# One 512-column up product per tile in an expert loop, with the transposes of the next token rows ahead of those of the hidden rows

## The reference, cut to what matters

```
def expert_block(args):
    xb, e = args
    hb = jax.nn.silu(xb @ w_gate[e]) * (xb @ w_up[e])
    return hb @ w_down[e]
```

## Time and profile before

| | |
|---|---|
| three executions | 2432.01, 2435.06, 2433.85 us |
| median | 2433.85 us |
| profiled execution, first to last instruction | 2431.3 us |
| TensorE busy | 2224.0 us, 91% of the span |
| weight loads of TensorE | 1827.0 us, 75% |
| VectorE, ScalarE, GpSimd busy | 1337.8, 909.3, 606.1 us |
| mean granted TensorE clock | 0.959 of full |
| expert loop | about 847 to 2296 us of the span |

### The profile page before, as it was taken

The page is one execution under the profiler, slowest core; times in us unless marked ns, Lnnn a source line. Parts: engine busy times, 40 slices in busy tenths (PEclk is TensorE's granted clock), DMA queues, the critical chain, the costliest instruction groups (busy, mean ns, idle before and its releaser), DMA issues.

```text
span 2431.3 us, 36221 instructions
## 1 busy us (share of the span) xinstructions
PE 2224.0 (91%) x12032; PEld 1827.0 (75%) x12033; DVE 1337.8 (55%) x2246; ACT 909.3 (37%) x1335; POOL 606.1 (25%) x672
## 2 busy tenths in 40 slices
PE   8999899999998299999999999999999999999700
PEld 3443778878886288888898898888888988988600
DVE  3221348888878555444544544554445455444298
ACT  2221123223333245434534534534345345443143
POOL 1000035454444412111211111111212111111166
PEclk9999999999999599999999999999999999999955
DMA  5980233333433377665765765865667678656386
GB/s 217 289 281 0 80 143 128 126 127 119 142 123 122 124 232 235 182 183 172 241 184 170 245 180 169 241 198 164 178 177 236 189 223 245 181 173 174 78 297 239
DMA packets 128121, 438.13 MB, mean 180 GB/s; under 512 B 24624, under 2 KB 26672, under 8 KB 123952
## 3 DMA queue, kind: packets, MB, share of 16 engines
q1 hardware_dynamic: 88736, 301.72, 35.5%
q0 software_dynamic: 39344, 135.88, 22.5%
HBM read 326.33 MB, written 112.26 MB: 180 GB/s over the span
## 4 chain that ended last, share of the span: by engine, by line
PE 91%; POOL 3%; issue 3%; DVE 2%; DMA 1%; ACT 0%; SPq 0%; POOLq 0%; DVEq 0%
PE ps L859 37%; PE ps L889 18%; PE ps L746 15%; PE ps L683 5%; PE ps L845 3%; POOL fin_r L1489 3%; PE ps L728 2%; PE ps L702 2%; PE ps L780 2%; PE ps L852 2%; PE ps L637 1%; PE ps L767 1%; PE ps L687 1%; PE ps L646 1%; PE ps L742 0%
## 5 line engine op out<-in xcount | busy, mean ns | idle before, releaser
L1246 DVE TENSOR_TENSOR wgu_lo<-wraw,wgu_hi 128x1024 fp32r<-128x1024 f32 x256 | 299.6, 1221 | 176.0 <-ACT wgu_hi L981 156.5
L859 PE MATMUL ps<-wgu_hi,mxT_hi 128*128 128x256 f32 (+1 forms) x1920 | 338.9, 319 | 1.6 <-DVE mxT_lo L1276 1.6
L859 PE MATMUL ps<-wgu_lo,mxT_hi 128*128 128x256 f32 (+1 forms) x1920 | 337.8, 318 | 0.0
L859 PE MATMUL ps<-wgu_hi,mxT_lo 128*128 128x256 f32 (+1 forms) x1920 | 337.8, 318 | 0.0
L859 PEld LDWEIGHTS ps<-wgu_hi,mxT_hi 128*128 128x128 f32 x1920 | 290.9, 191 | 33.7 <-issue 2.4
L859 PEld LDWEIGHTS ps<-wgu_lo,mxT_hi 128*128 128x128 f32 x1920 | 285.3, 191 | 25.0
L859 PEld LDWEIGHTS ps<-wgu_hi,mxT_lo 128*128 128x128 f32 x1920 | 285.3, 191 | 24.9
L981 ACT CAST wgu_hi<-wraw 128x1024 fp32r<-128x1024 f32 x256 | 253.6, 1062 | 20.3 <-DMA wraw<-expert_w_up 20.3
L1289 DVE TENSOR_TENSOR hid<-sgate,ps 128x256 f32<-128x256 f32 x160 | 67.2, 420 | 337.0 <-PE ps L859 337.0
L1456 POOL DMA_INDIRECT sums<-yrow,sx x81 | 131.4, 1622 | 296.4 <-DVE yrow L1303 270.9
L1004 ACT CAST hidT_hi<-ps 128x256 fp32r<-128x256 f32 x160 | 59.6, 372 | 381.7 <-PE ps L852 381.7
(11 more groups left out here) (175 smaller groups left out, 3373.3 us busy)
## 6 DMA issues: line engine op xcount, KB each, us to landing
wraw<-expert_w_gate SPq DMA_DIRECT2D x128, 512.0 KB, 6.5
wraw<-expert_w_up SPq DMA_DIRECT2D x128, 512.0 KB, 4.2
wraw<-expert_w_down SPq DMA_DIRECT2D x128, 512.0 KB, 4.4
xch<-x SPq DMA_DIRECT2D x16, 1024.0 KB, 8.8
first_stage<-ych SPq DMA_DIRECT2D x16, 1024.0 KB, 9.6
yt<-first_stage SPq DMA_DIRECT2D x16, 1024.0 KB
fin_r<-sums SPq DMA_DIRECT2D x32, 512.0 KB, 4.0
out<-fin_r SPq DMA_DIRECT2D x32, 512.0 KB, 2.9
```

Source lines behind the costliest of these rows:

```text
L859: mm = nc.tensor.matmul(ps, mxT[l][:, c, :], wgu[b][r][:, m, c, lo:hi], start=(n == 0 and c == 0), stop=(n == 2 and c == CH - 1))
L1246: nc.vector.tensor_tensor(lo, wraw[:, j % SLOTS, :], hi.bitcast(F32), ALU.subtract).then_inc(wlo_ok, 1)
```

## The change

The up product of a tile becomes one product of 24 matmuls of 512 columns in bank 1, with one semaphore `u_ps` in place of `ua_ps` and `ub_ps`. VectorE waits for it once and then makes both halves of `hid`. TensorE runs all eight x transposes directly behind the up product and the four hidden transposes behind those. The other engines' programs stay as they are.

```diff
-        psU = bank[1][:, 0:F // 2], bank[7][:, 0:F // 2]
+        psU = bank[1]
...
                 pe.wait_ge(wlo_ok, PIECES * e + GU_PIECES)
-                up_or_gate(psU[0], b, 1, 0, F // 2).then_inc(ua_ps, 1)
-                up_or_gate(psU[1], b, 1, F // 2, F).then_inc(ub_ps, 1)
+                up_or_gate(psU, b, 1, 0, F).then_inc(u_ps, 1)
+                pe.wait_ge(xrow_in, 16 * t + 32)
+                turn_x(0, x0_ps)
+                turn_x(1, x1_ps)
                 pe.wait_ge(hida_ok, t + 1)
                 turn_hidden(0, h0_ps)
-                pe.wait_ge(xrow_in, 16 * t + 32)
-                turn_x(0, x0_ps)
                 pe.wait_ge(hidb_ok, t + 1)
                 turn_hidden(1, h1_ps)
-                turn_x(1, x1_ps)
                 pe.wait_ge(wlo_ok, PIECES * e + PIECES)
...
-                for half, done, ok in ((0, ua_ps, hida_ok), (1, ub_ps, hidb_ok)):
+                dve.wait_ge(u_ps, t + 1)
+                dve.wait_ge(silu_ok, t + 1)
+                for half, ok in ((0, hida_ok), (1, hidb_ok)):
                     cols = slice(half * F // 2, (half + 1) * F // 2)
-                    dve.wait_ge(done, t + 1)
-                    if half == 0:
-                        dve.wait_ge(silu_ok, t + 1)
-                    nc.vector.tensor_tensor(hid[:, cols], sgate[:, cols], psU[half],
+                    nc.vector.tensor_tensor(hid[:, cols], sgate[:, cols], psU[:, cols],
                                             ALU.mult).then_inc(ok, 1)
```

More of the change, by code:

```diff
@@ L364, in trunk_kernel @@
         xrow_in, y_out, ixg_ok, sx_ok = sem("xrow_in"), sem("y_out"), sem("ixg_ok"), sem("sx_ok")
-        g_ps, ua_ps, ub_ps, x0_ps, x1_ps, xh_ev, xlo_ev = (
-            sem(n) for n in ("g_ps", "ua_ps", "ub_ps", "x0_ps", "x1_ps", "xh_ev", "xlo_ev"))
+        g_ps, u_ps, x0_ps, x1_ps, xh_ev, xlo_ev = (
+            sem(n) for n in ("g_ps", "u_ps", "x0_ps", "x1_ps", "xh_ev", "xlo_ev"))
         silu_ok, hida_ok, hidb_ok, h0_ps, h1_ps, hh_ev, hl_ev = (
```

## The result

| | before | changed |
|---|---|---|
| median | 2434.66 us (2432.01 to 2438.66, 5 executions) | 2445.24 us (2442.06 to 2446.67, 5 executions) |
| ratio to before | | 1.0039, 95% interval 1.0028 to 1.0050 |
| profiled span | 2431.3 us | 2444.9 us |

The changed kernel is slower, by 10.6 us of medians; the forecast was 10.4 (2444 us, worked out from 2433.85). By the interval the loss is 0.28 to 0.50%.

What follows compares the result with a forecast made beforehand. TensorE's own chain, repeated over 80 tiles, was taken to bound the kernel. Per tile -0.31 + 0.44 = +0.13 us, times 80 = +10.4 us, on the median 2433.85 gives 2444 us; range 2435 to 2455.

Steps and rivals of the forecast that it cites:

- Term 1: Up product: 24 matmuls of 512 columns take the gate's 5.44 us in place of 5.75, 0.31 us less per tile.
- rival E: Up product: 256-column matmuls carry no extra per-matmul cost, so merging gains nothing; 35 us slower, 2469 us; chance 0.02.
- Term 2: Hand-over from up to down: down's first weight load waits for ScalarE's cast of the hidden rows, 0.44 us more per tile.
- B: Hand-over to down closes sooner, its exposed weight load and two releases vanishing: 6.4 us faster, 2427 us; chance 0.05.
- C: Hand-over to down: one of those costs comes back, mainly the 0.11 us weight load; +1.6 us, 2435.5 us; chance 0.16.
- D: x transposes wait for a late gather in up to seven tiles, up to 13 us, 2457 us; chance 0.10.
- F: TensorE's clock drops in the loop after longer, partly idle transpose stretches; one tile in ten could cost over 100 us; chance 0.01.

Runs made afterwards that it cites:

- the last two runs: Gate product in two halves of 256 columns: on the kernel before, 2531.52 us (ratio 1.0399); on the changed kernel, 2471.27 us (ratio 1.0153).
- the run with the waits ahead: Kernel with hidden rows in quarters, TensorE's waits for down weights and last down read-out moved ahead of the first x transpose: 2408.66 us, ratio 0.9889.
- the run with quarters: Merged up product, hidden rows made, transposed and cast in four 128-column pieces between the last x transposes, against the kernel before: 2415.62 us, ratio 0.9922.

## Why the prediction was right

| step | forecast | changed kernel |
|---|---|---|
| up stretch | 5.44 | 5.45 us |
| eight x transposes | T0 + 0.88 | + 0.87 (1518.77 to 1519.64) |
| ScalarE starts its cast | + 1.30 | + 1.29 (1520.06) |
| release after the cast | 0.06 | 0.04 (chain of waits) |
| first weight load of down | + 1.73 | + 1.71 (1520.48) |
| tile | 18.19 | 18.18 us |
| 80 tiles | +10.4 | +10.6 us (medians) |

*Term 1* was right for the reason given. The gate product was a sound model of the merged up product, and the last two runs show that the cost goes with the columns of a matmul and not with a bank: rival E is dead. The gain of 0.06 that the Trainium skill's figures for an isolated matmul gave (TensorE: Matmul & The Clock Gate, "Back-to-back issue gap") is measured as 0.30.

*Term 2* was right in mechanism and size: 0.41 us from matmul start to matmul start (0.42 for the weight loads), where 0.44 was forecast. The two halves of the change were taken apart on the chip and don't simply add: the order alone costs 36.5 us, the merge alone 26.7, and both together 10.6. The stretch is the later of two chains, TensorE's transposes and the way of the hidden rows over VectorE, TensorE and ScalarE. Each half of the change lengthens the stretch by itself, and only the merge has a gain to set against it.

*Luck.* The total agrees to 0.2 us, which is closer than the method allows: 0.01 us in a row is 0.8 us over 80 tiles, and the interval of the ratio spans 6.8 to 12.2 us. Term 1 was 0.01 too large, term 2 0.03, and the two errors have opposite signs in the sum. The sign and the size of about 10 us are not luck; the 0.2 is.

*Steps sized wrongly that cost nothing.* Half 1 of `hid` was put at T0 + 1.04; VectorE makes both halves in 0.75 us, so it is ready at 0.95, and its transposes had no wait. ScalarE's two casts take 0.65 together, not 0.74. The wait of TensorE for `hidT_hi` was announced as some 0.35 us and 25 to 30 in all; the profile gives 0.24 for matmuls (19.4 in all) and 0.48 for weight loads (38.4), the two ways of counting one standstill; neither is inside 25 to 30.

*Rivals.* B did not occur: the first down group still takes 1.03 us from start to start (1520.49 to 1521.52) as in the earlier trace rows, so the weight load stays exposed after the wait. C is outside the interval of the ratio: its 1.6 us would be 1.0007, the interval begins at 1.0028. D did not occur either. The shortest lead of a gather is now

```profile
1839.93 0.99 POOL L1446 DMA_INDIRECT xrow<-h_rows,ixg  x1 [0.93 <-POOL ixg L1465]
1846.13 1.04 PE L845 MATMUL ps<-cst,xrow 128*128 128x128 f32 x8
```

that is 6.2 us, as the 6.1 of the earlier trace rows and not the 5.6 that was feared, and only the first gather of all is waited for. Shorter leads did occur in two of the experiments. With six x transposes first, two gathers had 5.51 and 5.55 us, and no matmul waited for them. In the run with the waits ahead the shortest was 5.07:

```profile
1494.65 0.99 POOL L1445 DMA_INDIRECT xrow<-h_rows,ixg  x1 [0.95 <-POOL ixg L1464]
1499.72 0.82 PE L845 MATMUL ps<-cst,xrow 128*128 128x128 f32 x5 [0.27 <-DMA xrow<-h_rows,ixg]
```

It cost 0.27 us, once. So a late gather can hold TensorE here, but D priced it with a landing of 7.5 us, and leads of 5.51 and 5.55 us, which are shorter than the feared 5.6, cost nothing. F did not occur: the clock is 1.00 in the loop and 0.958 over the run, against 0.959.

## What to carry to other kernels

Before merging two products to save matmuls, ask what the first one's early end was hiding: here 0.30 us of TensorE were bought with 0.41 of a chain over two other engines that had lain under it. The remedy was not to undo the merge but to shorten the chain to its first consumer: hand over the smallest piece that the next product's first weight load needs, and put other work of the same engine between the pieces. Then look at the waits that stand between the last of them and the consumer: here, once nothing else was late, moving them ahead was worth another 7 us.

## What the runs showed that I had not expected

Waits that are long satisfied cost time by where they stand. In the run with quarters they lay between short transposes and down, and the stretch was 1.33 us in kind-1 tiles and up to 1.46 in kind-0 tiles; ahead of the x transposes it was 1.29 in both, 7 us of the total. That register instructions hold the sequencer there is the reading that fits the cure and the 30 longer stretches, all in kind-0 tiles inside the loop and none outside it; the profile has no row that names it.

A longer loop body can cost far more than its instructions. With 132 matmuls per tile in place of 108, times the six tile bodies in the loop over a pair of experts, the instruction queue moved 152 packets in place of 24, and TensorE waited up to 8.6 us at each of the fourteen jumps back, 56 us in all, with 16 more for the lower clock that followed; with 108 there were 24 packets and none of those waits, in the same form of the gate product. The cause, a body too long to be kept from one turn to the next, is argued from the packets and from the place of the waits; where the limit lies was not measured, nor why some waits take 1.4 us and others 7.
